# A hybrid decoder layer on one core: where weight slots and activations begin, modulo 128 bytes

## The chip, the core and the metric

The kernel runs on one NeuronCore of one Trainium2 chip. The metric is the device time of one execution in microseconds, as a median of runs. The engines are TensorE (PE, with its weight loads shown apart as PEld), VectorE (DVE), ScalarE (ACT), GpSimd (POOL, here only a queue for DMAs) and SyncE (SP, the other DMA queue).

## The reference, cut to what matters

One layer on a prompt of 2048 tokens and on 32 sample tokens, width 1024, all float32:

```
h = rms_norm(x, g_mix_pre);  z = h @ w_in                      # 1024 -> 2048
y_a, y_b, y_c, y_d = pool(z), conformer_conv(z), spatial_gating(z), short_conv(z)
o = concat(y_a, y_b, y_c, y_d) @ w_out                         # 1024 -> 1024
x = x + rms_norm(o, g_mix_post)
f = rms_norm(x, g_ffn_pre)
f = square(relu(f @ w_up)) @ w_down                            # 1024 -> 4096 -> 1024
x = x + rms_norm(f, g_ffn_post)
```

The results are the new x for both token groups and the last rows that each mixer keeps.

## The kernel before, in words

The tokens go in four blocks b of 512; the last block also takes the 32 sample tokens (544 columns). Every weight matrix goes in panels of 256 columns, 1024 rows deep (K = 8 row tiles k of 128), 1 MB each. The list `order` names all panels j in the order in which every engine goes through them. There are 32 I panels (stage 1: w_in, eight per block), and then for each block four O panels (w_out) and four quarters q, each with four U panels (w_up) and four D panels (w_down). Between blocks the first D panel of the last quarter and the O panels of the next block are interleaved.

Products are made in three passes. A float32 weight is split into w_hi (ACT, `split_hi`, L677) and w_lo = raw - w_hi (DVE, `split_lo`, L1127), an activation into act_hi and act_lo (or u_hi and u_lo, the squared-ReLU result). `three` (L1773 to L1775) issues hi x hi, hi x lo and lo x hi into one PSUM bank; every matmul has its own weight load. What stands in the array (the second argument) and what moves over it (the third) depends on the panel:

- In I panels (but for the last) and in U panels w stands, 128 columns of it, and act moves: 512 columns, or 256 and 288 in the last block's U panels.
- In D panels u stands, 128 tokens of it, and w moves, 256 columns. In O panels act stands and w moves. In the last I panel of a block, called VV, and in the sample rows that each I panel of block 0 ends with, act stands and w moves too.

There are two weight slots, panel j uses slot j % 2, and a slot is filled again when panel j - 2 is done. In block 0 of stage 1 the two halves of w_in are also written to DRAM (L610, L611), and blocks 1 to 3 load them from there by POOL's queue (L619, L620), w_hi and w_lo of a panel one after the other. In all other panels the raw weight is loaded by SP and split.

The mixers' results come back from DRAM as mixc, and `mix_part` writes them into act_hi (ACT, L900) and act_lo (DVE, L1432) for the O panels. In block 0 ACT waits there for tiles of the last VV panel, which still reads act. The normalised f then overwrites act for the U panels.

Of the kernel before, what the change touches and what calls it, by code (L numbers as in the profile page):

```python
# [5 lines left out]
def hybrid_trunk_step(nc, x_prompt, x_sample, state_pool, state_conv, state_short, g_mix_pre, g_mix_post,  # L6
# [7 lines left out]
    fp32, f32r, bf16 = mybir.dt.float32, mybir.dt.float32r, mybir.dt.bfloat16  # L14
# [85 lines left out]
    with ctx:  # L100
# [12 lines left out]
        wlo_d = nc.dram_tensor("wlo_scratch", [NI, P, K, PC], f32r, kind="Internal").ap()  # L113

        raw = sb("raw", [P, 2, K, PC])
        w_hi = sb("w_hi", [P, 2, K, PC], f32r)
        w_lo = sb("w_lo", [P, 2, K, PC], f32r)
        ident = sb("ident", [P, P])
        cst = sb("cst", [P, NROW])
        eps = sb("eps", [P, 1])  # L120
# [4 lines left out]
        sgu_gb = sb("sgu_gb", [NS, PC])  # L125
        wpool = sb("wpool", [P, 2, P])
        headmean = sb("headmean", [P, P])
        inv_cnt = sb("inv_cnt", [P, 2, HP + 1])
        v_small = sb("v_small", [P, 3, 4 * NCH])
        vs_small = sb("vs_small", [NS, 3, 4])  # L130

        junk = sb("junk", [P, D], bf16)
        junk_o = sb("junk_o", [P, PC], bf16)
        junk_y = sb("junk_y", [P, PC], bf16)
        warm = sb("warm", [P, 1])
        x_stats = sb("x_stats", [P, 3, NCH])
        xms, xroot, xinv = (x_stats[:, i, :] for i in range(3))


        act_hi = sb("act_hi", [P, K, NX], f32r)  # L140
        act_lo = sb("act_lo", [P, K, NX], f32r)


        sms = sb("sms", [NS, 3])
        oms = sb("oms", [P, NCH + 1, NP])
        osum = sb("osum", [P, NCH + 1])
# [59 lines left out]
        us_sb = sb("us_sb", [P, 2, NS], to=p1)  # L206
        bs_sb = sb("bs_sb", [P, 2, NS], to=p1)
        gate_s = sb("gate_s", [P, 2, NS], to=p1)
        s_gate = v_raw[:, :, :].rearrange("p a c -> p (a c)").rearrange("p (t n) -> p t n", t=2)

        sgu_w_sb = v_n[:, 0:2, :].rearrange("p a c -> p (a c)").rearrange("p (h t) -> p h t", h=4)
# [323 lines left out]
        def _(pool):  # L535
# [71 lines left out]

            for j in range(NI):
                pool.wait_ge(lo_ready, split_no[j])
                pool.dma_start(whi_d[j], w_hi[:, j % 2, :, :]).then_inc(parts_out[j % 2], 16)  # L610
                pool.dma_start(wlo_d[j], w_lo[:, j % 2, :, :]).then_inc(parts_out[j % 2], 16)  # L611
            store(0, 0, ya_done, pool_d[:, :, :])
            for j in part_no:
                _, b, _, p = order[j]
                s = j % 2
                wait_panel(pool, j - 2)
                if j in (NI, NI + 1):
                    pool.wait_ge(parts_out[s], 32 * (NI // 2))
                pool.dma_start(w_hi[:, s, :, :], whi_d[p]).then_inc(part_full[s], 16)  # L619
                pool.dma_start(w_lo[:, s, :, :], wlo_d[p]).then_inc(part_full[s], 16)  # L620
# [47 lines left out]
        def _(act):  # L668
            def split_hi(j):
                if j >= NPAN:  # L670
                    return
                s = j % 2
                act.wait_ge(raw_full[s], 16 * raw_no[j])
                wait_panel(act, j - 2)
                if 2 <= j < NI:
                    act.wait_ge(parts_out[s], 32 * (j // 2))
                SC.activation(w_hi[:, s, :, :], raw[:, s, :, :], ACT.Copy).then_inc(hi_ready, 1)  # L677

            def x_stat(n):

# [211 lines left out]
            def mix_part(b, i):  # L892
                m = no(b, i)
                _, t0, n = tiles_of(b)[i]
                act.wait_ge(mix_full[m % 2], 16 * (m // 2 + 1))
                if b == 0:
                    act.wait_ge(tile_done, 2 * J2 - 1 + i // 2)
                else:
                    wait_panel(act, index("U", b - 1, Q - 1, NP - 1))
                SC.activation(act_hi[:, :, t0:t0 + n], mixc[:, m % 2, :, 0:n], ACT.Copy).then_inc(mix_hi, 1)  # L900

            def o_squares(j, i):
                _, b, _, p = order[j]
# [215 lines left out]
        def _(dve):  # L1119
            def split_lo(j):  # L1120
                if j >= NPAN:
                    return
                s = j % 2
                dve.wait_ge(hi_ready, split_no[j])
                if 2 <= j < NI:
                    dve.wait_ge(parts_out[s], 32 * (j // 2))
                DVE.tensor_tensor(w_lo[:, s, :, :], raw[:, s, :, :], w_hi[:, s, :, :].bitcast(fp32), ALU.subtract)\  # L1127
# [300 lines left out]
            def mix_part(b, i):  # L1428
                m = no(b, i)
                _, t0, n = tiles_of(b)[i]  # L1430
                dve.wait_ge(mix_hi, m + 1)
                DVE.tensor_tensor(act_lo[:, :, t0:t0 + n], mixc[:, m % 2, :, 0:n],  # L1432
                                  act_hi[:, :, t0:t0 + n].bitcast(fp32), ALU.subtract).then_inc(mix_lo, 1)

            def o_copy(j, i):
                _, b, _, p = order[j]
# [334 lines left out]
        def _(pe):  # L1771
# [139 lines left out]
            for b in range(NB):  # L1911
                for jj in range(NI):
                    j, s = NI * b + jj, jj % 2
                    wait_weights(j)
                    for t in range(2):
                        bank = mm[2 * s + t]
                        if jj >= 2:
                            pe.wait_ge(frees[jj], 2 * b + t + 1)
                        elif b > 0:
                            pe.wait_ge(frees[jj], 2 * (b - 1) + t + 1)  # L1920
                        if jj != VV:
                            if jj == 0 and t == 0:
                                pe.wait_ge(h_hi_ready, 2 * NCH * (b + 1))
                                pe.wait_ge(h_lo_ready, 2 * NCH * (b + 1))
                            c = slice(t * P, (t + 1) * P)
                            for k in range(K):
                                last_mm = three(bank[:, :], w_hi[:, s, k, c], w_lo[:, s, k, c],
                                                act_hi[:, k, 0:N1], act_lo[:, k, 0:N1], k)
                            last_mm.then_inc(tile_done, 1)
                            if b == 0 and jj == 0 and t == 0:  # L1930
                                small_parts()
                            if b == NB - 1 and jj == UV and t == 0:
                                last_rows()
                        else:
                            for half in range(2):
                                n = 2 * t + half
                                r = slice(n * P, (n + 1) * P)
                                for k in range(K):
                                    last_mm = three(bank[:, half * PC:(half + 1) * PC], act_hi[:, k, r],
                                                    act_lo[:, k, r], w_hi[:, s, k, :], w_lo[:, s, k, :], k)  # L1940
# [8 lines left out]
                    if b == 0:  # L1949
                        if jj == 0:  # L1950
                            pe.wait_ge(smp_hi, 1)
                            pe.wait_ge(smp_lo, 1)
                            pe.wait_ge(bias_ready, 1)
                        if jj >= 2:
                            pe.wait_ge(zs_ready, jj - 1)
                        for k in range(K):
                            last_mm = three(mm[4 + s][0:NS, 0:PC], act_hi[:, k, N1:NX], act_lo[:, k, N1:NX],
                                            w_hi[:, s, k, :], w_lo[:, s, k, :], k)
# [85 lines left out]
            for j in range(J2, NPAN):  # L2044
# [3 lines left out]
                if kind == "U":  # L2048
# [4 lines left out]
                    for t in range(2):  # L2053
                        c = slice(t * P, (t + 1) * P)
                        for c0, c1 in halves(b):
                            bank = take_bank(j, i)
                            for k in range(K):
                                last_mm = three(mm[bank][:, 0:c1 - c0], w_hi[:, s, k, c], w_lo[:, s, k, c],
                                                act_hi[:, k, c0:c1], act_lo[:, k, c0:c1], k)
                            last_mm.then_inc(bank_done[bank], 1)  # L2060
                            i += 1
                else:
                    hi, lo = (act_hi, act_lo) if kind == "O" else (u_hi, u_lo)
                    for i, bank_tiles in enumerate(token_banks(b)):
                        bank = take_bank(j, i)
                        for h, (tile, t0, n) in enumerate(bank_tiles):
                            for k in range(K):
                                if kind == "O" and p == 0 and k == 0:
                                    pe.wait_ge(mix_lo, no(b, tile) + 1)
                                if kind == "D" and p == 0 and i == 0 and h == 0:  # L2070
                                    pe.wait_ge(u_lo_ready, u_no(b, q, k, len(halves(b))))
                                last_mm = three(mm[bank][0:n, h * PC:(h + 1) * PC], hi[:, k, t0:t0 + n],
                                                lo[:, k, t0:t0 + n], w_hi[:, s, k, :], w_lo[:, s, k, :], k)
# [61 lines left out]
```

## Time and profile before

| | |
|---|---|
| median of 3 runs | 2232.03 us (2230.04 to 2232.41) |
| profiled execution | 2230.47 us, its span 2228.2 us |
| granted TensorE clock, mean | 0.983 |
| PE busy | 2122.0 us (95%), 14425 instructions |
| PEld busy | 1932.4 us (87%) |
| DVE busy | 1083.2 us (49%) |
| ACT busy | 754.6 us (34%) |
| DMA | 287.42 MB, mean 129 GB/s |

The span runs from the first to the last recorded instruction, and the execution's own time is 2.3 us longer. A matmul's duration in the records includes the time in which it drains while the next one is already under way, so a stream of matmuls is measured by the distance of their starts. A few matmul records can be missing, which does not move the starts of the others.

### The profile page before, as it was taken

What the parts mean: (1) busy time and instruction counts of PE and PEld (TensorE: products, weight loads), DVE (VectorE), ACT (ScalarE), POOL (GpSimd) and SP (SyncE); (2) the same over time, 40 slices, a digit from 0 to 9 for tenths busy, and PEclk for the clock granted to TensorE, in tenths of its full rate; (3) what the DMA queues carried; (4) which work ended last, traced back from release to release, by engine and by line L of the source; (5) the groups of instructions that cost most, each with busy time, mean ns of one, the idle gap of its engine ahead of it and who ended that gap; (6) DMA issues with size and microseconds to landing.
All of it is one profiled execution on the core that took longest, in us unless ns stands there. A gap on an engine that the chain in (4) does not pass through costs nothing.

```text
span 2228.2 us, 33002 instructions
## 1 busy us (share of the span) xinstructions
PE 2122.0 (95%) x14425; PEld 1932.4 (87%) x14425; DVE 1083.2 (49%) x1404; ACT 754.6 (34%) x1159; POOL 107.6 (5%) x190
## 2 busy tenths in 40 slices
PE   6999999994999999999999999999999989999997
PEld 5887778784798898989899898889899989999997
DVE  3687786866523334563333346533334553333334
ACT  4424232234233223443322344332324432314132
POOL 2011111110000000000000000000000000000000
PEclk9999999997899999999999999999999999999999
DMA  7754646553132223444233344533334333222231
GB/s 250 277 201 165 222 170 209 194 178 129 59 114 95 95 95 114 139 150 153 94 107 95 97 132 152 170 95 95 95 95 135 108 103 116 77 93 78 77 95 41
DMA packets 184836, 287.42 MB, mean 129 GB/s; under 512 B 5967, under 2 KB 162292, under 8 KB 176484
## 3 DMA queue, kind: packets, MB, share of 16 engines
q1 hardware_dynamic: 160868, 169.99, 23.9%
q0 software_dynamic: 22784, 114.28, 14.6%
q8 instruction: 114, 1.87, 0.3%
q10 hardware_dynamic: 1040, 1.05, 0.1%
q14 instruction: 30, 0.25, 0.0%
HBM read 245.01 MB, written 40.57 MB: 128 GB/s over the span
## 4 chain that ended last, share of the span: by engine, by line
PE 83%; DVE 7%; ACT 4%; DMA 3%; issue 2%; POOL 0%; ACTq 0%; POOLq 0%; DVEq 0%
PE mm L1773 27%; PE mm L1775 27%; PE mm L1774 27%; ACT w_hi L677 2%; DVE w_lo L1127 2%; DMA mixc<-mixT_scratch 1%; DVE conv L1171 1%; PE tr L1778 1%; DMA x_in<-in_x_prompt 1%; DMA raw<-in_w_in 1%; PE tr L2002 1%; ACT junk_y L976 0%; PE mm L1833 0%; PE tr L1799 0%; DVE f_sb L1516 0%
## 5 line engine op out<-in xcount | busy, mean ns | idle before, releaser
L1127 DVE TENSOR_TENSOR w_lo<-raw,w_hi 128x2048 fp32r<-128x2048 f32 x152 | 348.4, 2292 | 696.4 <-ACT w_hi L677 696.4
L1773 PE MATMUL mm<-act_hi,w_hi 128*128 128x512 f32 (+2 forms) x1728 | 632.2, 366 | 11.1 <-DVE act_lo L1484 5.8
L1775 PE MATMUL mm<-act_hi,w_lo 128*128 128x512 f32 (+2 forms) x1728 | 632.3, 366 | 0.0
L1774 PE MATMUL mm<-act_lo,w_hi 128*128 128x512 f32 (+2 forms) x1728 | 625.9, 362 | 0.0
L1773 PE MATMUL mm<-w_hi,u_hi 128*128 128x256 f32 (+1 forms) x2176 | 603.2, 277 | 1.7 <-DVE u_lo L1500 0.9
L1774 PE MATMUL mm<-w_lo,u_hi 128*128 128x256 f32 (+1 forms) x2176 | 600.8, 276 | 0.0
L1775 PE MATMUL mm<-w_hi,u_lo 128*128 128x256 f32 (+1 forms) x2176 | 600.8, 276 | 0.0
L677 ACT ACTIVATE w_hi<-raw 128x2048 fp32r<-128x2048 f32 x152 | 290.8, 1913 | 579.1 <-PE mm L1775 572.9
L1773 PEld LDWEIGHTS mm<-w_hi,u_hi 128*128 128x128 f32 (+1 forms) x2176 | 398.2, 183 | 4.9 <-DVE u_lo L1500 3.8
L1774 PEld LDWEIGHTS mm<-w_lo,u_hi 128*128 128x128 f32 (+1 forms) x2176 | 398.3, 183 | 1.1
L1775 PEld LDWEIGHTS mm<-w_hi,u_lo 128*128 128x128 f32 (+1 forms) x2176 | 398.2, 183 | 0.7
L1773 PEld LDWEIGHTS mm<-act_hi,w_hi 128*128 128x128 f32 x1728 | 328.3, 190 | 62.9 <-issue 14.9
L1774 PEld LDWEIGHTS mm<-act_lo,w_hi 128*128 128x128 f32 x1728 | 328.2, 190 | 57.1 <-issue 2.4
L1775 PEld LDWEIGHTS mm<-act_hi,w_lo 128*128 128x128 f32 x1728 | 327.5, 190 | 50.5
L1773 PE MATMUL mm<-w_hi,act_hi 128*128 128x256 f32 (+1 forms) x736 | 205.9, 280 | 7.0 <-DVE act_lo L1432 4.3
L1774 PE MATMUL mm<-w_lo,act_hi 128*128 128x256 f32 (+1 forms) x736 | 203.9, 277 | 0.0
L1775 PE MATMUL mm<-w_hi,act_lo 128*128 128x256 f32 (+1 forms) x736 | 203.9, 277 | 0.0
L949 ACT ACTIVATE square<-mm 128x512 f32<-128x512 f32 (+2 forms) x160 | 81.8, 511 | 257.7 <-PE mm L1775 255.1
L1171 DVE SCALAR_TENSOR_TENSOR conv<-g_ext,cst,conv 128x512 f32<-128x512 f32 x240 | 163.0, 744 | 0.7 <-ACT conv L800 0.7
L1498 DVE CAST u_hi<-square 128x512 fp32r<-128x512 f32 (+2 forms) x160 | 60.0, 375 | 187.6 <-ACT square L951 187.6
L1773 PEld LDWEIGHTS mm<-w_hi,act_hi 128*128 128x128 f32 (+1 forms) x736 | 131.2, 178 | 9.4 <-issue 5.1
L1774 PEld LDWEIGHTS mm<-w_lo,act_hi 128*128 128x128 f32 (+1 forms) x736 | 131.2, 178 | 2.0 <-issue 0.5
(244 smaller groups left out, 1341.7 us busy)
## 6 DMA issues: line engine op xcount, KB each, us to landing
raw<-in_w_ffn_up SPq DMA_DIRECT2D x64, 1024.0 KB, 5.4
raw<-in_w_ffn_down SPq DMA_DIRECT2D x64, 1024.0 KB, 5.2
w_hi<-whi_scratch POOLq DMA_DIRECT2D x24, 1024.0 KB, 5.2
w_lo<-wlo_scratch POOLq DMA_DIRECT2D x24, 1024.0 KB, 7.9
raw<-in_w_out SPq DMA_DIRECT2D x16, 1024.0 KB, 5.2
whi_scratch<-w_hi POOLq DMA_DIRECT2D x8, 1024.0 KB, 8.6
wlo_scratch<-w_lo POOLq DMA_DIRECT2D x8, 1024.0 KB, 10.8
mixc<-mixT_scratch POOLq DMA_DIRECT2D x16, 512.0 KB, 5.8
```

Of the source, the lines that this page charges most:

```text
L677: SC.activation(w_hi[:, s, :, :], raw[:, s, :, :], ACT.Copy).then_inc(hi_ready, 1)
L949: SC.activation(square[:, at % 2, 0:c1 - c0], mm[bank][:, 0:c1 - c0], ACT.Relu).then_inc(bank_free[bank], 1)
L1127: DVE.tensor_tensor(w_lo[:, s, :, :], raw[:, s, :, :], w_hi[:, s, :, :].bitcast(fp32), ALU.subtract)\
L1171: DVE.scalar_tensor_tensor(out=c, in0=g_ext[:, t, k:k + N1], scalar=col("conv_w", 2 * k + t), in1=c, op0=ALU.mult, op1=ALU.add).then_inc(c ...
L1498: DVE.tensor_copy(u_hi[:, k, c0:c1], square[:, at % 2, 0:c1 - c0]).then_inc(u_hi_ready, 1)
L1773: PE.matmul(out, whi, xhi, start=(k == 0), stop=False)
L1774: PE.matmul(out, whi, xlo, start=False, stop=False)
L1775: return PE.matmul(out, wlo, xhi, start=False, stop=(k == K - 1))
L1778: PE.matmul(bank[:, 0:n], headmean[:, :], src, start=True, stop=True).then_inc(done, 1)
L2002: last = PE.transpose(tr[hh][:, kk * P:kk * P + n], f_sb[0:n, m % 2, k * P:(k + 1) * P], ident[0:n, 0:n])
```

## The change

The change gives each panel's weights an address within their slot by the panel's kind, and gives act two addresses within its buffer, one for the stage in which it moves and one for the O panels, in which it stands. A slot becomes 2064 elements (8256 bytes) per partition instead of 2048, an act buffer 4368 instead of 4352. Six small tensors are allocated at another place, so that act_hi begins at 0 and act_lo at 64 modulo 128. One wait of `mix_part` in block 0 asks for a tile more, since the shifted tile reaches 64 bytes into its neighbour. The diff, without the lines that only put `w_hi(j)` for `w_hi[:, s, :, :]` and `mix_act_hi` for `act_hi`:

```diff
-        w_hi = sb("w_hi", [P, 2, K, PC], f32r)
-        w_lo = sb("w_lo", [P, 2, K, PC], f32r)
+        PITCH = K * PC + P // 8
+        w_hi_slots = sb("w_hi", [P, 2 * PITCH], f32r)
+        w_lo_slots = sb("w_lo", [P, 2 * PITCH], f32r)
...
-        inv_cnt = sb("inv_cnt", [P, 2, HP + 1])
-        v_small = sb("v_small", [P, 3, 4 * NCH])
-        vs_small = sb("vs_small", [NS, 3, 4])
...
+        act_hi_buf = sb("act_hi", [P, K * NX + P // 8], f32r)
+        act_lo_buf = sb("act_lo", [P, K * NX + P // 8], f32r)
+
+        act_hi, mix_act_hi = (act_hi_buf[:, o:o + K * NX].rearrange("p (k t) -> p k t", k=K) for o in (0, P // 8))
+        act_lo, mix_act_lo = (act_lo_buf[:, o:o + K * NX].rearrange("p (k t) -> p k t", k=K) for o in (P // 8, 0))
+
+        def in_slot(slots, j):
+
+            base = (j % 2) * PITCH
+            off = base + (-base if order[j][0] in "OD" else P // 8 - base) % (P // 4)
+            return slots[:, off:off + K * PC].rearrange("p (k c) -> p k c", k=K)
+
+        def w_hi(j):
+            return in_slot(w_hi_slots, j)
+
+        def w_lo(j):
+            return in_slot(w_lo_slots, j)
...
         x_stats = sb("x_stats", [P, 3, NCH])
         xms, xroot, xinv = (x_stats[:, i, :] for i in range(3))
-
-
-        act_hi = sb("act_hi", [P, K, NX], f32r)
-        act_lo = sb("act_lo", [P, K, NX], f32r)
...
-                SC.activation(w_hi[:, s, :, :], raw[:, s, :, :], ACT.Copy).then_inc(hi_ready, 1)
+                SC.activation(w_hi(j), raw[:, s, :, :], ACT.Copy).then_inc(hi_ready, 1)
...
-                    act.wait_ge(tile_done, 2 * J2 - 1 + i // 2)
+
+                    act.wait_ge(tile_done, 2 * J2 - 1 + min(i, 1))
...
-                SC.activation(act_hi[:, :, t0:t0 + n], mixc[:, m % 2, :, 0:n], ACT.Copy).then_inc(mix_hi, 1)
+                SC.activation(mix_act_hi[:, :, t0:t0 + n], mixc[:, m % 2, :, 0:n], ACT.Copy).then_inc(mix_hi, 1)
...
-                    hi, lo = (act_hi, act_lo) if kind == "O" else (u_hi, u_lo)
+                    hi, lo = (mix_act_hi, mix_act_lo) if kind == "O" else (u_hi, u_lo)
```

Where the operands of a matmul begin, in bytes modulo 128, in the two built programs (a row of w is 1024 bytes, a row of act or u 2176 = 17 x 128, and every tile within a row begins at a multiple of 512, so the same offset holds for all tiles):

| panel | before: moves, stands | changed: moves, stands |
|---|---|---|
| I but for VV, U | act 64, w 0 | act 0, w 64 |
| VV, and the sample rows of stage 1 | w 0, act 64 | w 64, act 0 |
| O | w 0, act 64 | w 0, act 64 |
| D | w 0, u 64 | w 0, u 64 |

On every engine the instructions, their order and the semaphores that they wait for are the same in both programs; only addresses differ, and the value of the one wait.

## Rows read from the trace of the kernel before

**Rows 1.** The page, parts 2 (40 slices) and 4 (the chain).
```profile
PEclk9999999997899999999999999999999999999999
...
PE mm L1773 27%; PE mm L1775 27%; PE mm L1774 27%; ACT w_hi L677 2%; DVE w_lo L1127 2%; DMA mixc<-mixT_scratch 1%; DVE conv L1171 1%; PE tr L1778 1%; DMA x_in<-in_x_prompt 1%; DMA raw<-in_w_in 1%; PE tr L2002 1%; ACT junk_y L976 0%; PE mm L1833 0%; PE tr L1799 0%; DVE f_sb L1516 0%
```

**Rows 2.** Groups by form, L1773: form, xcount | busy us, mean ns | idle before.
```profile
L1773 PE MATMUL mm<-w_hi,u_hi 128*128 128x256 f32 x2048 | 567.9, 277 | 1.7 <-DVE u_lo L1500 0.9
...
L1773 PE MATMUL mm<-act_hi,w_hi 128*128 128x512 f32 x1216 | 484.4, 398 | 6.9 <-DVE act_lo L1160 5.3 <-DVE act_lo L1484 1.6
...
L1773 PE MATMUL mm<-w_hi,act_hi 128*128 128x256 f32 x640 | 179.3, 280 | 7.0 <-DVE act_lo L1432 4.3 <-DVE w_lo L1127 2.7
...
L1773 PE MATMUL mm<-act_hi,w_hi 128*128 128x288 f32 x256 | 75.2, 294 | 0.0
...
L1773 PE MATMUL mm<-act_hi,w_hi 128*128 128x256 f32 x256 | 72.5, 283 | 4.2 <-DVE act_lo L1484 4.2
```

**Rows 3.** PE in order of time (start, us): four U panels, first and last of 192.
```profile
1062.04 0.39 PE L1773 MATMUL mm<-act_hi,w_hi 128*128 128x512 f32 x1
...
1105.96 0.39 PE L1775 MATMUL mm<-act_hi,w_lo 128*128 128x512 f32 x1
```

**Rows 4.** Busy PE, PEld, DVE, ACT, POOL, clock, DMA, GB/s: four U panels.
```profile
1062.04:1106.19 44.15, 44.15 (x194) 36.07 (x193) 16.74 (x18) 16.42 (x19) 0.00 (x0) 1.00 0.30 96
```

**Rows 5.** PE in order of time: one D panel, first and last of 96.
```profile
1894.34 0.28 PE L1773 MATMUL mm<-w_hi,u_hi 128*128 128x256 f32 x1
...
1905.11 0.28 PE L1775 MATMUL mm<-w_hi,u_lo 128*128 128x256 f32 x1
```

**Rows 6.** The same: last block's U panel, 24 of 288 and 24 of 256.
```profile
1910.74 0.29 PE L1773 MATMUL mm<-act_hi,w_hi 128*128 128x288 f32 x1
...
1913.91 0.28 PE L1773 MATMUL mm<-act_hi,w_hi 128*128 128x256 f32 x1
...
1916.60 0.28 PE L1775 MATMUL mm<-act_hi,w_lo 128*128 128x256 f32 x1
```

**Rows 7.** The same: 24 of the sample rows, and 48 of VV.
```profile
69.06 0.28 PE L1773 MATMUL mm<-w_hi,act_hi 128*32 128x256 f32 x1
...
71.68 0.28 PE L1775 MATMUL mm<-w_hi,act_lo 128*32 128x256 f32 x1
...
128.62 0.28 PE L1773 MATMUL mm<-w_hi,act_hi 128*128 128x256 f32 x1
...
133.95 0.28 PE L1775 MATMUL mm<-w_hi,act_lo 128*128 128x256 f32 x1
```

**Rows 8.** DVE in order of time.
```profile
476.95 1.22 DVE L1432 TENSOR_TENSOR act_lo<-mixc,act_hi 128x1024 fp32r<-128x1024 f32 x1
...
481.75 1.22 DVE L1189 TENSOR_TENSOR v_n<-v_raw,v_small 128x1024 f32<-128x1024 f32 x1
```

**Rows 9.** POOL and PE in order of time, and landing times of the page, part 6.
```profile
215.48 0.53 POOL L619 DMA_DIRECT2D w_hi<-whi_scratch  x1 [12.26 <-PE mm L1775]
...
228.31 0.79 PE L1773 MATMUL mm<-act_hi,w_hi 128*128 128x512 f32 x1
...
w_lo<-wlo_scratch POOLq DMA_DIRECT2D x24, 1024.0 KB, 7.9
...
raw<-in_w_in SPq DMA_DIRECT2D x7, 1024.0 KB, 9.2
```

**Rows 10.** ACT in order of time, end of stage 1.
```profile
464.54 0.60 ACT L702 ACTIVATE v_raw<-mm 128x512 f32<-128x512 f32 x1 [4.84 <-PE mm L1775]
465.03 1.99 ACT L900 ACTIVATE act_hi<-mixc 128x1024 fp32r<-128x1024 f32 x2
```

**Rows 11.** Waits of DVE in stage 1: us in total, times, longest.
```profile
DVE g_ext L1280 <- ACT p_raw L702: 28.8, 6, 6.1
```

**Rows 12.** Waits of PE from 560 us on.
```profile
PE tr L2002 <- DVE act_lo L1484: 6.2, 6, 1.9
...
PE tr L1778 <- DVE conv_s L1679: 2.6, 1, 2.6
```

More of the change, by code:

```diff
@@ L208, in hybrid_trunk_step @@
         gate_s = sb("gate_s", [P, 2, NS], to=p1)
+        inv_cnt = sb("inv_cnt", [P, 2, HP + 1], to=p1)
+        v_small = sb("v_small", [P, 3, 4 * NCH], to=p1)
+        vs_small = sb("vs_small", [NS, 3, 4], to=p1)
         s_gate = v_raw[:, :, :].rearrange("p a c -> p (a c)").rearrange("p (t n) -> p t n", t=2)
@@ L609, in _ @@
                 pool.wait_ge(lo_ready, split_no[j])
-                pool.dma_start(whi_d[j], w_hi[:, j % 2, :, :]).then_inc(parts_out[j % 2], 16)
-                pool.dma_start(wlo_d[j], w_lo[:, j % 2, :, :]).then_inc(parts_out[j % 2], 16)
+                pool.dma_start(whi_d[j], w_hi(j)).then_inc(parts_out[j % 2], 16)
+                pool.dma_start(wlo_d[j], w_lo(j)).then_inc(parts_out[j % 2], 16)
             store(0, 0, ya_done, pool_d[:, :, :])
@@ L618, in _ @@
                     pool.wait_ge(parts_out[s], 32 * (NI // 2))
-                pool.dma_start(w_hi[:, s, :, :], whi_d[p]).then_inc(part_full[s], 16)
-                pool.dma_start(w_lo[:, s, :, :], wlo_d[p]).then_inc(part_full[s], 16)
+                pool.dma_start(w_hi(j), whi_d[p]).then_inc(part_full[s], 16)
+                pool.dma_start(w_lo(j), wlo_d[p]).then_inc(part_full[s], 16)
                 if p == 0:
@@ L1126, in split_lo @@
                     dve.wait_ge(parts_out[s], 32 * (j // 2))
-                DVE.tensor_tensor(w_lo[:, s, :, :], raw[:, s, :, :], w_hi[:, s, :, :].bitcast(fp32), ALU.subtract)\
+                DVE.tensor_tensor(w_lo(j), raw[:, s, :, :], w_hi(j).bitcast(fp32), ALU.subtract)\
                    .then_inc(lo_ready, 1)
@@ L1431, in mix_part @@
                 dve.wait_ge(mix_hi, m + 1)
-                DVE.tensor_tensor(act_lo[:, :, t0:t0 + n], mixc[:, m % 2, :, 0:n],
-                                  act_hi[:, :, t0:t0 + n].bitcast(fp32), ALU.subtract).then_inc(mix_lo, 1)
+                DVE.tensor_tensor(mix_act_lo[:, :, t0:t0 + n], mixc[:, m % 2, :, 0:n],
+                                  mix_act_hi[:, :, t0:t0 + n].bitcast(fp32), ALU.subtract).then_inc(mix_lo, 1)
             def o_copy(j, i):
@@ L1926, in _ @@
                             for k in range(K):
-                                last_mm = three(bank[:, :], w_hi[:, s, k, c], w_lo[:, s, k, c],
+                                last_mm = three(bank[:, :], w_hi(j)[:, k, c], w_lo(j)[:, k, c],
                                                 act_hi[:, k, 0:N1], act_lo[:, k, 0:N1], k)
@@ L1939, in _ @@
                                     last_mm = three(bank[:, half * PC:(half + 1) * PC], act_hi[:, k, r],
-                                                    act_lo[:, k, r], w_hi[:, s, k, :], w_lo[:, s, k, :], k)
+                                                    act_lo[:, k, r], w_hi(j)[:, k, :], w_lo(j)[:, k, :], k)
                                 if half == 1:
@@ L1957, in _ @@
                             last_mm = three(mm[4 + s][0:NS, 0:PC], act_hi[:, k, N1:NX], act_lo[:, k, N1:NX],
-                                            w_hi[:, s, k, :], w_lo[:, s, k, :], k)
+                                            w_hi(j)[:, k, :], w_lo(j)[:, k, :], k)
                         last_mm.then_inc(zs_done, 1)
@@ L2057, in _ @@
                             for k in range(K):
-                                last_mm = three(mm[bank][:, 0:c1 - c0], w_hi[:, s, k, c], w_lo[:, s, k, c],
+                                last_mm = three(mm[bank][:, 0:c1 - c0], w_hi(j)[:, k, c], w_lo(j)[:, k, c],
                                                 act_hi[:, k, c0:c1], act_lo[:, k, c0:c1], k)
@@ L2072, in _ @@
                                 last_mm = three(mm[bank][0:n, h * PC:(h + 1) * PC], hi[:, k, t0:t0 + n],
-                                                lo[:, k, t0:t0 + n], w_hi[:, s, k, :], w_lo[:, s, k, :], k)
+                                                lo[:, k, t0:t0 + n], w_hi(j)[:, k, :], w_lo(j)[:, k, :], k)
                             if h == len(bank_tiles) - 1:
```

## The prediction

> **What bounds the kernel now.** I read the page first. TensorE's granted clock is at nine tenths or more in 38 of 40 slices [rows 1]; in a stage of four U panels it is 1.00, the 2.4 GHz level, with PE busy all of it [rows 4]. The chain that ended last is 81% matmuls of three lines, L1773 to L1775 [rows 1]. So the kernel is worth what one matmul is worth, times their number. The groups by form, the second view, give that number: each of the three lines issues (L1773 shown) 1216 matmuls of 512 moving columns with act moving, 256 of 288 and 256 of 256 columns with act moving, 2048 of 256 columns with a weight moving over u, and 640 with a weight moving over act [rows 2]. The duration there (398 or 277 ns) overlaps with the next matmul and is no cost. The cost is the pitch, from one start to the next, which is read in the order of time.
>
> Pitch, third view, each from two starts and the matmuls between them:
> - D panel (w moves from offset 0 modulo 128, u stands at 64), 96 matmuls of 256 columns: (1905.11 - 1894.34) / 95 = 113.4 ns [rows 5].
> - U panels (act moves from 64, w stands at 0), 192 matmuls of 512 columns: (1105.96 - 1062.04) / 191 = 229.9 ns [rows 3].
> - U panels of the last block, same offsets: 256 columns (1916.60 - 1913.91) / 23 = 117.0 ns, 288 columns (1913.91 - 1910.74) / 24 = 132.1 ns [rows 6].
> - VV panel of stage 1 (w moves from 0, act stands at 64), 48 matmuls: (133.95 - 128.62) / 47 = 113.4 ns. Sample rows (w moves from 0, a stationary tile of only 32 columns), 24: (71.68 - 69.06) / 23 = 113.9 ns [rows 7].
>
> Here is the pattern on which the forecast rests. 512 columns cost 229.9 = 2 x 113.4 + 3.2. 256 columns from offset 64 cost 117.0 = 113.4 + 3.6. 288 columns: 113.4 x 288/256 = 127.5, and 4.6 more. So a matmul that moves from 0 costs 113.4 ns per 256 columns and nothing fixed, and one that moves from 64 costs the same per column and 3 to 5 ns more, once. The size of the standing tile does not matter (113.9 at 32 columns, 113.4 at 128). Nothing else waits in these stretches: PE is busy 44.15 of 44.15 us [rows 4].
>
> **The change part by part.**
> 1. U panels and the first seven columns of stage 1 (w_hi, w_lo stand, act moves). Standing goes from 0 to 64, moving from 64 to 0. That is the pair of offsets that the D panels already have. By the pattern the fixed part goes. 512 columns: 3 x 1216 = 3648 matmuls x 3.2 ns = 11.7 us. 256 columns in the last block: 768 x 3.6 ns = 2.8 us. 288 columns: 768 x 4.6 ns = 3.5 us. Together 18.0 us. The saving at 512 columns with act from 0 is in no row of before. It is bounded below by nothing (the pitch has to do with the form and not the offset), above by a price per column: if a column from 0 cost only what the 2.4 GHz level asks, 0.417 ns, and 113.4 - 106.7 = 6.7 ns were fixed, then 512 columns would take 220.0 ns and each saves 9.9 ns, 36.1 us in all. I take 3.2, since the step from 256 to 512 columns from offset 64 (229.9 - 117.0 = 112.9) is already what 256 columns from offset 0 cost as a whole.
> 2. The VV panel of each block in stage 1, and the sample rows of stage 1. The slot is chosen by the kind of panel, and these are of kind I though the weight moves in them. So here w moves from 64 and act stands at 0: the worse pair. VV is 4 panels x 4 tiles x 8 x 3 = 384 matmuls, the sample rows 8 x 8 x 3 = 192; 576 x 3.2 = 1.8 us lost.
> 3. O and D panels. w moves from 0 and the stationary (the shifted copy of act, or u) stands at 64, as before: no change, and these are more than half of all, 3 x 2048 for D and 3 x (640 - 128) for O without the sample rows [rows 2]. The transposes and head statistics read tiles that keep their offsets.
> 4. ACT's and DVE's splits now write at 64 for I and U panels. A DVE operation of 1024 elements takes 1.22 us on act and mixc, at offset 64, and 1.22 us on v_raw and v_n, at offset 96 [rows 8], so I take no change. They lie beside a panel of 48 x 0.23 = 11 us and take some 2 us each, which hides a tenth more as well; uncovered, a tenth would be 0.2 us in each of the panels.
> 5. POOL's loads of w_hi and w_lo in stage 1 write 8 KB rows that begin at 64. A pair is issued from 215.48 on, and its panel begins at 228.31: 12.8 us for what takes 0.5 + 7.9 = 8.4 [rows 9]. Some 4 us of slack hide it. No row shows a load that begins at 64; the nearest are w_in's 1 MB loads in the crowded first stage at 9.2 us [rows 9], 1.3 longer, also hidden. I take 0.
> 6. The new wait: in block 0 ACT's second mixing tile waits for one more tile of the last VV panel. Behind it on ACT are two more such tiles, and DVE and the first O panel wait for them. But ACT evacuates that very tile into v_raw at 464.54, ahead of both, and starts the two at 465.03 [rows 10]. The wait is fulfilled when it is reached: 0.
> 7. What a faster PE meets. In stage 1 DVE waits for what ACT takes from PE's results (28.8 us before g_ext alone [rows 11]), so it follows. PE's own waits for DVE from 560 us on are small, the largest 6.2 us in six parts at the block edges [rows 12]; they hang on chains that begin with the end of a PE panel, so they move and do not grow. Only where DVE itself is the chain (the step from block 0 to 1, and the 2.6 us before conv_s [rows 12]) a faster panel becomes a longer wait: 48 + 40 matmuls x 3.2 ns, 0.3 us.
>
> Sum: 18.0 - 1.8 - 0.3 = 15.9 us saved. The profiled execution took 2230.5 us (span 2228.2 and 2.3 around it): 2214.6. The median of the runs is 2232.0, 1.6 above the profiled one, so the forecast is 2216.2.
>
> A rule that speaks against this, in sentences that the sum does not use. The Trainium skill, "TensorE: Matmul & The Clock Gate", section "Back-to-back issue gap", gives a warm pitch of N/2.4 + 2.5 ns with no term for an address: 215.8 ns at 512 columns, where the trace has 229.9, and 109.2 at 256, where it has 113.4 and 117.0. By that rule the sum would be 0; the trace does not agree with it in either form. "SBUF — State Buffer", section "DMA port swizzle", puts the memory's lines at 16 bytes: offsets 64 and 0 would both begin a line and the change would give nothing. The 3 to 5 ns between forms of equal width [rows 5 and 6] are not what that rule leads one to expect, but the forms differ in more than the offset, so it is rival 2 below.
>
> **Rivals.**
> 1. The offset costs per column, not once. Then 512 columns go to 220.0 ns (36.1 us), 256 save 2.8, 288 columns go to 113.4 + 32 x 0.417 = 126.7 (5.5 x 768 = 4.2): 43.1 - 1.8 - 0.3 = 41.0 us, 2191. For it: TensorE at the full level needs no more per column. Against it: 288 columns from 64 cost 4.6 extra and 512 cost 3.2, which does not grow with width.
> 2. The 3 ns belong to the form and not the offset. In rows 5 and 7 a weight moves (1 KB rows), in rows 3 and 6 act moves (rows of 2176 bytes). In this kernel of before, form and offset never part, so no row excludes it. Then nothing changes: 2232, or 2234 if VV alone pays. A change that does not do what it says would end here too.
> 3. Slower: the loads of stage 1 decide. 24 pairs have to land within 12.8 us and take 8.4. Rows that begin in mid-line would have to stretch them 1.5-fold before anything shows; at 1.9-fold, 16.0 us, each pair holds PE 3.2 us, 24 x 3.2 = 77, less the 16 saved: 2293. At 1.65-fold, 13.9 us, it is 26 - 16 = 10 us slower, 2242. Against it: even the crowded loads are below the limit. Nothing speaks for it but that no row shows it.
>
> **How the numbers follow.** My forecast 0.60 (2212 to 2221 for its own range: the 3.2 can't be read better than by some 0.5 ns, and the 3.6 and 4.6 by 0.6). Rival 1 0.12, rival 2 0.18, rival 3 or some other loss 0.10. The range from 2190 to 2233 holds the forecast, rival 1 with what lies between, and most of rival 2; it leaves out rival 3 and the rest of rival 2, whose two ends (2232 and 2234) lie about its edge. A measurement of this kernel tells 0.2%, 4.5 us, from no change: faster 0.72, same 0.18, slower 0.10.
>
> **What would show it.** In the profile after: 192 matmuls of 512 columns in a U stage at a pitch of 226.7 ns (229.9 again is rival 2, 220 rival 1); 256 and 288 columns in the last block at 113.4 and 127.5; D and O unchanged at 113.4; the VV panel up to 116.6 and the sample rows with it (unchanged there, and the standing offset or the form has a part in it). POOL's pairs landing above 12 us, or PE waiting at the head of stage 1's panels, would be rival 3. I am wrong if the pitch of U stays, or if it falls and the waits at the block edges grow by as much.

## The result: slower by 1.3%, and the profile after

The changed kernel takes 2260.28 us (median of 4 runs, 2258.81 to 2262.45) against 2231.03 us of the kernel before in the same series (median of 4 runs): a ratio of 1.0132, with a 95% interval of 1.0114 to 1.0149. The forecast was 2216.2 us with a range of 2190 to 2233. It was wrong in its sign.

These lines of the changed kernel's page give its busy times and granted clock. They answer to the table of times and to [rows 1]:

```profile
span 2258.2 us, 33002 instructions
...
PE 2157.9 (96%) x14425; PEld 1958.8 (87%) x14425; DVE 1083.3 (48%) x1404; ACT 754.4 (33%) x1159; POOL 107.6 (5%) x190
...
PEclk9999999997999999999999999999999999999999
```

The same instructions ran, and DVE, ACT and POOL took the same time for them. PE alone was busy longer: 2157.9 - 2122.0 = 35.9 us. Its idle time shrank from 106.2 to 100.3 us, and 35.9 - 5.9 is the 30.0 us by which the span grew. So nothing new is waited for. The granted clock is no reason either, since its mean rose a little, from 0.983 to 0.985. The matmuls themselves follow each other more slowly. The largest group by form, the matmuls of the D panels, shows it faintly, since durations overlap (line, form, count | busy, mean ns | idle before; it answers to the first row of [rows 2]):

```profile
L1791 PE MATMUL mm<-w_hi,u_hi 128*128 128x256 f32 x2048 | 573.9, 280 | 0.9
```

The starts show it fully. Below is PE of the changed kernel (start and duration, us), the first and last matmul of each stretch: four U panels (192, as [rows 3]), one D panel (96, as [rows 5]), 24 of 288 and 24 of 256 columns in the last block ([rows 6]), a VV panel (48) and sample rows (24, both [rows 7]):

```profile
1072.90 0.39 PE L1791 MATMUL mm<-act_hi,w_hi 128*128 128x512 f32 x1
...
1117.24 0.39 PE L1793 MATMUL mm<-act_hi,w_lo 128*128 128x512 f32 x1
...
1903.68 0.28 PE L1791 MATMUL mm<-w_hi,u_hi 128*128 128x256 f32 x1
...
1914.77 0.28 PE L1793 MATMUL mm<-w_hi,u_lo 128*128 128x256 f32 x1
...
1934.52 0.29 PE L1791 MATMUL mm<-act_hi,w_hi 128*128 128x288 f32 x1
...
1937.56 0.30 PE L1793 MATMUL mm<-act_hi,w_lo 128*128 128x288 f32 x1
1937.69 0.28 PE L1791 MATMUL mm<-act_hi,w_hi 128*128 128x256 f32 x1
...
1940.44 0.29 PE L1793 MATMUL mm<-act_hi,w_lo 128*128 128x256 f32 x1
...
130.06 0.28 PE L1791 MATMUL mm<-w_hi,act_hi 128*128 128x256 f32 x1
...
135.60 0.28 PE L1793 MATMUL mm<-w_hi,act_lo 128*128 128x256 f32 x1
...
69.69 0.28 PE L1791 MATMUL mm<-w_hi,act_hi 128*32 128x256 f32 x1
...
72.39 0.28 PE L1793 MATMUL mm<-w_hi,act_lo 128*32 128x256 f32 x1
```

The next table has the pitch, that is the distance of two starts, before and after. "By the pitch" is its change times the number of matmuls.

| stretch | before, ns | after, ns | matmuls | forecast, us | by the pitch, us |
|---|---|---|---|---|---|
| D and O | 113.4 | 116.7 | 8160 | 0 | +27 |
| U and I, 512 columns | 229.9 | 232.1 | 3648 | -11.7 | +8 |
| U, 256 columns | 117.0 | 119.6 | 768 | -2.8 | +2 |
| U, 288 columns | 132.1 | 132.2 | 768 | -3.5 | 0 |
| VV | 113.4 | 117.9 | 384 | +1.2 | +1.7 |
| sample rows of stage 1 | 113.9 | 117.4 | 192 | +0.6 | +0.7 |

(For instance D: (1914.77 - 1903.68) / 95 = 116.7.) The last column adds up to 39.4 us, but the span grew by 30.0 only. Of the difference, 5.9 us is the idle time that PE lost: a slower stream arrives later at a point at which PE waited anyway. The rest, by an estimate, is in the clock. For short stretches both traces have a granted clock of 0.50, the 1.2 GHz level, where 512-column matmuls start (261.68 - 259.54) / 5 = 428 ns apart instead of 230:

```profile
259.54 0.63 PE L1773 MATMUL mm<-act_hi,w_hi 128*128 128x512 f32 x1
...
261.68 0.63 PE L1775 MATMUL mm<-act_hi,w_lo 128*128 128x512 f32 x1
```

In the changed kernel less of PE's work fell into such stretches. From 500 to 620 us, for instance, the granted clock (third value from the end) was 0.82 before, which is the first of these rows, and 0.84 after, which is the second:

```profile
500.00:620.00 120.00, 85.84 (x475) 73.32 (x475) 72.37 (x154) 45.18 (x81) 6.94 (x11) 0.82 0.26 89
500.00:620.00 120.00, 86.32 (x482) 72.83 (x479) 73.09 (x152) 46.68 (x80) 6.92 (x11) 0.84 0.28 91
```

Over the whole span PE was busy at the 1.2 GHz level for 32.6 us before and for 26.9 us after. By an estimate from these two numbers, half of the 5.7 us came back, 2.9 us. The sum is then 39.4 - 5.9 - 2.9 = 30.6 us, against 30.0 measured. The largest term is one that the forecast had at zero: panels whose operands keep their offset modulo 128.

What does not keep its value is the address modulo 256. The addresses of w_hi and w_lo, of act_hi and act_lo, and of u_hi and u_lo in the two built programs give this table, where k is the row tile:

| modulo 256 | before | changed, slot 0 | changed, slot 1 |
|---|---|---|---|
| D, O: w_hi, w_lo (move) | 128, 128 | 128, 0 | 0, 128 |
| D: u_hi, u_lo (stand), even k | 192, 192 | 192, 192 | 192, 192 |
| U, I: w_hi, w_lo (stand) | 128, 128 | 192, 64 | 192, 64 |
| U, I: act_hi, act_lo (move), even k | 192, 192 | 0, 128 | 0, 128 |

(Rows of act and u are 8.5 x 256 bytes, so at odd k they lie 128 further.) The weight buffers became 16512 bytes, an odd multiple of 128, so w_lo and w_hi no longer agree modulo 256. In D and O panels, where w moves, they are 128 apart.

### The profile page after: what moved, and what is told of

It is laid out like the page before. It is cut to its first block, busy times and chain, and to the rows that moved or that the text cites. A ratio compares the mean times of both kernels' runs of the same rounds, so it can differ in the third digit from the quotient of the medians.

```text
span 2258.2 us, 33002 instructions
## 1 busy us (share of the span) xinstructions
PE 2157.9 (96%) x14425; PEld 1958.8 (87%) x14425; DVE 1083.3 (48%) x1404; ACT 754.4 (33%) x1159; POOL 107.6 (5%) x190
## 4 chain that ended last, share of the span: by engine, by line
PE 85%; DVE 7%; ACT 4%; DMA 2%; issue 2%; POOL 0%; ACTq 0%; DVEq 0%; POOLq 0%
PE mm L1791 28%; PE mm L1792 28%; PE mm L1793 27%; DVE w_lo L1145 1%; ACT w_hi L694 1%; DMA mixc<-mixT_scratch 1%; DVE conv L1189 1%; PE tr L1796 1%; DMA raw<-in_w_in 1%; DMA x_in<-in_x_prompt 1%; PE tr L2020 0%; PE mm L1851 0%; PE tr L1817 0%; ACT junk_y L994 0%; DVE o_sb L1484 0%
## 5 line engine op out<-in xcount | busy, mean ns | idle before, releaser
L1792 PE MATMUL mm<-act_lo,w_hi 128*128 128x512 f32 (+2 forms) x1728 | 632.4, 366 | 0.0
L1791 PE MATMUL mm<-w_hi,u_hi 128*128 128x256 f32 (+1 forms) x2176 | 609.6, 280 | 0.9
L1792 PE MATMUL mm<-w_lo,u_hi 128*128 128x256 f32 (+1 forms) x2176 | 607.8, 279 | 0.0
L1792 PEld LDWEIGHTS mm<-w_lo,act_hi 128*128 128x128 f32 (+1 forms) x736 | 131.6, 179 | 2.2 <-issue 0.5
```

The lines of the kernel that those rows point to most:

```text
L1791: PE.matmul(out, whi, xhi, start=(k == 0), stop=False)
L1792: PE.matmul(out, whi, xlo, start=False, stop=False)
```

## The experiments

### The streams alone, and each part of the change alone

**m1_pairs** leaves the layer out and has no engine but TensorE at work while the streams run. Its core follows, with `at` giving a place by its byte address, and two of the 52 lines of its table (columns, standing columns, moving hi, lo and row pitch, standing hi, lo and row pitch, step, groups):

```diff
+            ('D before s0', 256, 128, 32896, 49280, 1024, 169920, 187328, 2176, 512, 4),
+            ('D after s0', 256, 128, 32896, 49408, 1024, 169920, 187328, 2176, 512, 4),
...
+                        last = three(bank[0:m, 0:n], at(sh + g % 4 * step + k * s_p, m),
+                                     at(sl + g % 4 * step + k * s_p, m),
+                                     at(mh + k * mp, n), at(ml + k * mp, n), k)
```

> A program of TensorE streams alone: it copies one block of x over the whole SBUF and then issues the three-pass pattern of a D or a U panel for 52 choices of the four operands' addresses; nothing of the layer is computed. Each stream is four groups of 24 matmuls (two at 512 columns). Theory A (the pitch depends only on the operands' addresses, and the address modulo 256 counts: the kernel before has w_hi and w_lo both at 128 modulo 256, the changed one has one at 0 and one at 128): the streams with the addresses of before run at 113.4 (D) and 229.9 ns (U), those of the changed kernel at 116.8 and 232.2, and w_lo moved alone by 128 bytes gives 116.8, by 256 bytes 113.4. Rival B (the slower pitch is an effect of the whole program, of other engines or of instruction supply): all D streams have one pitch and no address changes it. Rival C (only the offset modulo 128 of what moves counts, as the prediction had it): w_lo at +64 costs, at +128 it does not.

PE of m1 in order of time, first and last of 96 (the first is followed late, after 200 ns): D with the addresses of before, D with those of the changed kernel, D with w_lo 256 bytes further, D with both halves of w 64 bytes further:

```profile
48.15 0.36 PE L115 MATMUL mm<-mem 128*128 128x256 f32 x1
...
59.03 0.28 PE L117 MATMUL mm<-mem 128*128 128x256 f32 x1
...
70.19 0.36 PE L115 MATMUL mm<-mem 128*128 128x256 f32 x1
...
81.36 0.28 PE L117 MATMUL mm<-mem 128*128 128x256 f32 x1
...
240.01 0.36 PE L115 MATMUL mm<-mem 128*128 128x256 f32 x1
...
250.89 0.28 PE L117 MATMUL mm<-mem 128*128 128x256 f32 x1
...
318.12 0.36 PE L115 MATMUL mm<-mem 128*128 128x256 f32 x1
...
329.50 0.28 PE L117 MATMUL mm<-mem 128*128 128x256 f32 x1
```

The stretches last 10.88, 11.17, 10.88 and 11.38 us. Without the first three matmuls the pitches are, in ns (256-column D streams, then 512-column U streams; each operand moved by so many bytes from the addresses of before; slots 0 and 1 are the two weight slots):

```
D  as before 113.5 (both slots)   as changed 116.7, 116.7 (slots 0, 1)   32 standing columns 113.5
D  w_lo moved    +16 118.3  +32 118.0  +64 118.8  +96 117.9  +128 116.7  +192 117.8  +256, 512 .. 4096 113.5
D  w_hi and w_lo +16 119.1  +32 118.4  +64 118.9  +128 113.4  +192 118.9  +256 113.3
D  u_hi and u_lo +16 117.8  +32 117.0  +64 118.9  +128 113.6  +192 118.9  +256 113.5
D  u_lo alone    +64 116.6  +128 113.8  +256 113.5
U  as before 230.0, 230.5 (slots)   as changed 232.3 (both)
U  act both -64 232.1  -128 229.8  -192 232.3  -256 230.2;  act_lo -64 231.6  -128 231.1  -256 230.0
U  w both +64 232.3  +128 230.0  +192 232.1  +256 230.0;    w_lo +64 231.8  +128 230.7  +256 230.0
```

The D streams and those of 512 columns repeat the pitch that they have in the kernel, before and after, with nothing else running. Rivals B and C fall: addresses alone make it, and +128 costs. Theory A holds in its numbers (113.5, 116.7, and 113.5 again at 256). The exception is U's 256 columns: 117.8 ns in m1 for the addresses of before and of after alike, but 117.0 and 119.6 in the kernels, where 24 of them alternate with 24 of 288 columns. No run shows whether that is the reason.

**e1_act_only** has only act's half of the change and **e2_slots_only** only the weight slots' half. The core of each edit follows, against the changed kernel. A small unused tensor, left out here, keeps the other addresses in place.

```diff
-        PITCH = K * PC + P // 8
+        PITCH = K * PC
...
-            off = base + (-base if order[j][0] in "OD" else P // 8 - base) % (P // 4)
-            return slots[:, off:off + K * PC].rearrange("p (k c) -> p k c", k=K)
+            return slots[:, base:base + K * PC].rearrange("p (k c) -> p k c", k=K)
```

```diff
-        act_hi_buf = sb("act_hi", [P, K * NX + P // 8], f32r)
-        act_lo_buf = sb("act_lo", [P, K * NX + P // 8], f32r)
+        act_hi = mix_act_hi = sb("act_hi", [P, K, NX], f32r)
+        act_lo = mix_act_lo = sb("act_lo", [P, K, NX], f32r)
```

> Only act's part of the change: act_hi and act_lo at two offsets, the weight slots at the addresses modulo 256 of before (w_hi and w_lo 128, both slots). Theory A (D and O panels slowed since w_hi and w_lo, which move there, no longer agree modulo 256): D and O stay at 113.4 ns; the time lies near before, 2231, or as much above or below as U and I give: with act moving from 0 modulo 128 by the prediction's price 12 to 18 us faster, by the pitch of the changed kernel (232.2 at 512 columns) 8 to 10 us slower. Rival B (a whole-program effect of the change): a part of the 29 us stays in D and O although their operands' addresses are those of before.

> Only the weight slots' part of the change: slots 8256 bytes apart, w_lo's buffer 128 bytes further from w_hi's, act at the addresses of before (64 modulo 128, both halves). Theory A: D and O at 116.8 ns as in the changed kernel, 8160 matmuls x 3.4 ns = 28 us less what waits absorb, so 2250 to 2260 us; U's pitch shows what w standing at 64 does alone. Rival B or an effect of act's placement: D near 113.4 and the time near 2231.

e1: 2232.07 us, a ratio of 1.0001 (0.9991 to 1.0011). e2: 2259.63 us, 1.0125 (1.0109 to 1.0141). The slots alone are the whole loss. PE of e1 in order of time, one O panel of the last block, first and last of 96, and the VV panel of block 0, 48:

```profile
1703.00 0.28 PE L1791 MATMUL mm<-w_hi,act_hi 128*128 128x256 f32 x1
...
1713.76 0.28 PE L1793 MATMUL mm<-w_hi,act_lo 128*128 128x256 f32 x1
...
128.68 0.28 PE L1791 MATMUL mm<-w_hi,act_hi 128*128 128x256 f32 x1
...
134.27 0.28 PE L1793 MATMUL mm<-w_hi,act_lo 128*128 128x256 f32 x1
```

The O panel has 113.3 ns. VV has 118.9; there w still moves from 0, and act now stands at 0 modulo 128. In e2 an O panel and four U panels:

```profile
1720.38 0.28 PE L1790 MATMUL mm<-w_hi,act_hi 128*128 128x256 f32 x1
...
1731.47 0.28 PE L1792 MATMUL mm<-w_hi,act_lo 128*128 128x256 f32 x1
...
660.47 0.39 PE L1790 MATMUL mm<-act_hi,w_hi 128*128 128x512 f32 x1
...
704.81 0.40 PE L1792 MATMUL mm<-act_hi,w_lo 128*128 128x512 f32 x1
```

They have 116.7 and 232.1 ns, both as in the changed kernel. So the 2 ns that U lost also come from the slots. e1's U panels stay at 230.0 (192 from 660.16 to 704.09 us): with act moving from 0 and w standing at 0 there is neither the gain nor the loss that its expectation held possible.

### One buffer, 128 or 256 bytes further

```diff
         w_hi = sb("w_hi", [P, 2, K, PC], f32r)
+        gap = sb("gap", [P, 32])
         w_lo = sb("w_lo", [P, 2, K, PC], f32r)
```

(64 instead of 32 in w_lo_256. In both, three small tensors that the long streams do not read move to another place, so that act, u and all after them stay where they are.)

> The kernel before with one address changed: w_lo's buffer begins 128 bytes further, so w_hi lies at 128 and w_lo at 0 modulo 256, both still at 0 modulo 128; act, u and every offset modulo 128 stay (three small tensors move to make room, no matmul of the long stages reads them). Theory A (m1: the two halves of what moves must agree modulo 256): D and O at 116.7 ns instead of 113.4, 8160 x 3.3 = 27 us, U of 512 columns at 230.7, 3648 x 0.7 = 3 us, less some 4 us that waits absorb: 2255 to 2260, the whole of the changed kernel's loss from 128 bytes. Rival (the second slot's distance of 8320 bytes or the two offsets within the slots cause it): near 2231.

> The same with w_lo's buffer 256 bytes further instead of 128. Theory A: w_hi and w_lo agree modulo 256 again, D at 113.4 and U at 230.0, the time within 0.2% of before, 2231. Rival (any change of the distance between the buffers costs, their 16384 bytes being special): D at 116.7 and 2255 or more.

128 bytes: 2252.08 us, 1.0089 (1.0072 to 1.0106). 256 bytes: 2232.81 us, 1.0001 (0.9991 to 1.0010). PE of w_lo_128, a D panel (96), and of w_lo_256, an O panel (96):

```profile
1911.90 0.28 PE L1775 MATMUL mm<-w_hi,u_hi 128*128 128x256 f32 x1
...
1922.99 0.28 PE L1777 MATMUL mm<-w_hi,u_lo 128*128 128x256 f32 x1
```

```profile
1702.35 0.28 PE L1775 MATMUL mm<-w_hi,act_hi 128*128 128x256 f32 x1
...
1713.12 0.28 PE L1777 MATMUL mm<-w_hi,act_lo 128*128 128x256 f32 x1
```

They have 116.7 and 113.4 ns. A gap of 128 bytes makes 20 of the 29 us, and doubling it takes them back, with the small tensors moved alike in both. So the distance of w_lo from w_hi modulo 256 is shown as their cause. The expectation of 2255 to 2260 was 3 us too high. Its allowance for waits was right; what it lacked is the clock:

```profile
PE 2148.3 (95%) x14425; PEld 1955.2 (87%) x14425; DVE 1083.8 (48%) x1404; ACT 754.7 (34%) x1159; POOL 108.0 (5%) x190
```

With a span of 2250.2 us PE idled 101.9 us, 4.3 less than before, where some 4 were allowed. And PE was busy at the 1.2 GHz level for 24.8 us instead of 32.6, which by half of the difference gives 3.9 us, an estimate.

For the remaining 9 us the pitches give some 8, an estimate. U and I have 230.6 ns here (192 matmuls from 659.98 to 704.02 us) against 232.1 in the changed kernel, which is 5.5 us. U's 256 columns have 116.4 against 119.6 there, 2.5 us. e2 has the 232.1 with act at its old place, so the standing halves of w at +64 and +192 are behind the larger part.

### Is there a rule?

> Again TensorE streams alone, nothing of the layer computed; all rows and tiles keep one address modulo 256 unless said. m1 leaves two readings of the 113.4 and 118.9 ns of a 256-column matmul. Theory A1 (relation): what counts is the distance of moving and standing operand modulo 128; 64 apart gives 113.4 and equal gives 118.9, wherever they lie, and the two moving halves must agree modulo 256. Theory A2 (absolute): the moving operand has to lie at 0 modulo 128 and the standing one at 64. They part at moving 64, standing 0: A1 113.4, A2 118 or so. For 512 columns m1 never went below 229.8, with act's rows of 2176 bytes, which lie by turns at 0 and 128 modulo 256. If that turn costs (theory C), rows of 2048 or 2304 bytes bring 512 columns to 2 x 113.4 = 226.8 ns and 256 columns moved over 2176-byte rows stay at 117 to 118; if 512 columns have 3.2 ns of their own (rival), all row pitches give 230. The number of standing columns has no part in either.

The edit against m1 is another table: all addresses are multiples of 4096 plus the offset named. Pitches in ns follow, with m and s for the offsets of what moves and what stands. A row is as long as its columns unless said, and standing rows have 1024 bytes:

```
256 columns, s0:   m0 120.0  m32 116.6  m64 113.3  m96 120.0  m128 118.6  m160 117.4  m192 113.4  m224 118.4
256 columns, s64:  m0 117.8  m64 119.9  m128 117.7  m192 120.0;  m0 with standing rows of 2176 bytes: 113.8
512 columns, s0:   m0 226.6  m32 233.4  m64 229.1  m128 232.3  m192 233.4
512 columns, s64:  m0 233.4  m64 227.3  m192 233.4
512 columns, m64 s0, moving rows of 2176 bytes: 230.2;  of 2304: 228.9;  of 4096: 229.1
256 columns, m64 s0, moving rows of 2048, 2176, 2304 bytes: 117.8, 116.7, 117.8
288 columns, m64 s0: 132.3, 132.3, 131.6 (rows of 1152, 2176, 2304)
```

Both readings fail. "64 apart is fast" (A1) gives m0 s64 at 113.4; it is 117.8. "Moving at 0, standing at 64" (A2) gives m64 s0 as slow; it is the fastest at 113.3. At 512 columns equal offsets do best (226.6 and 227.3), and 64 apart costs 2 to 7 ns, the opposite of 256 columns. But they have to be equal modulo 256: m128 s0 has 232.3. Theory C fails too: neither 2048 nor 2304 bytes as such bring 226.8. What stays is that the pitch depends on offset, row pitch and width together, within a band of 113.3 to 120.9 and of 226.6 to 233.4 ns. (The 120.9 is m0 s64 with both low halves 128 bytes further.)

> TensorE streams alone, with the addresses of this kernel and of layouts that could be built into it. By m2, 512 columns take 226.6 ns where act's rows are 2048 bytes and act and w agree modulo 128; so act at 128 modulo 256 with rows of 2048 bytes over w at 128: 226.6 (before: 230.0). The VV panel with act there: near 120 (before 113.4), and 113.4 if w is moved to +64. For the last block's 256 and 288 columns m2 gives no rule; if any start of act does better than 117 and 132 it shows here. Rival: m2's 226.6 holds only for addresses that are whole multiples of 4096 as m2's were, and U stays at 229 to 230 here.

m3 has a third table, with this kernel's own addresses. Its 512 columns over w at 128 modulo 256 take, with act's rows of 2048 bytes, 226.8 ns for act at 128 modulo 256, 229.1 at 192, 232.3 at 0 and 233.4 at 64; as before 230.0. The rival, that 226.6 needs round addresses, falls. VV would pay 120.0 with such an act, and 117.8, not 113.4, with w moved by 64. 256 and 288 columns never beat 116.7 and 132.2 with rows of 2176 bytes. With act's rows of 2304 bytes and act at 64 modulo 256 the stream of 256 columns took 113.3; no kernel was built with that layout.

### Two kernels from what was found

**agree_256** keeps the offsets modulo 128 of the change and makes hi and lo agree modulo 256:

```diff
-        w_hi_slots = sb("w_hi", [P, 2 * PITCH], f32r)
-        w_lo_slots = sb("w_lo", [P, 2 * PITCH], f32r)
+        w_hi_slots = sb("w_hi", [P, 2 * K * PC + P // 2], f32r)
+        w_lo_slots = sb("w_lo", [P, 2 * K * PC + P // 2], f32r)
...
-            off = base + (-base if order[j][0] in "OD" else P // 8 - base) % (P // 4)
+            off = base + (-base if order[j][0] in "OD" else P // 8 - base) % (P // 2)
```

> The changed kernel with its offsets modulo 128 kept (what moves at 0, what stands at 64) and the halves made to agree modulo 256: w_hi's and w_lo's buffers 16640 bytes, the second slot at 8448 in O and D panels, act_lo a multiple of 256 bytes from act_hi (two small tensors move to make room). Theory A: all of the 29 us comes back, D and O at 113.4, U at 229.8 as m3's stream of that layout, so within 0.2% of 2232: the offsets modulo 128 as such give U nothing. Rival (the prediction's pattern after all, once the halves agree): U at 226.7 and 2216 to 2220.

2233.06 us, 1.0003 (0.9994 to 1.0012). Four U panels (192) and an O panel (96) of it:

```profile
661.50 0.40 PE L1793 MATMUL mm<-act_hi,w_hi 128*128 128x512 f32 x1
...
705.43 0.40 PE L1795 MATMUL mm<-act_hi,w_lo 128*128 128x512 f32 x1
...
1704.69 0.28 PE L1793 MATMUL mm<-w_hi,act_hi 128*128 128x256 f32 x1
...
1715.45 0.28 PE L1795 MATMUL mm<-w_hi,act_lo 128*128 128x256 f32 x1
```

They have 230.0 and 113.3 ns, the pitches of before. The idea of the change, carried out without its side effect, is worth nothing, and my pattern with it. (VV, where w moves from 64 here, has 113.4 ns, 48 matmuls from 129.87 to 135.20 us.)

**rows_2048** is the kernel before with act packed closely for the U panels of blocks 0 to 2:

```diff
+        act_hi_buf = sb("act_hi", [P, K * NX + 16], f32r)
+        act_lo_buf = sb("act_lo", [P, K * NX + 48], f32r)
...
+        act_hi = act_hi_buf[:, 16:16 + K * NX].rearrange("p (k t) -> p k t", k=K)
+        act_lo = act_lo_buf[:, 0:K * NX].rearrange("p (k t) -> p k t", k=K)
+        f_act_hi = act_hi_buf[:, 0:K * N1].rearrange("p (k t) -> p k t", k=K)
+        f_act_lo = act_lo_buf[:, 48:48 + K * N1].rearrange("p (k t) -> p k t", k=K)
```

> The kernel before with another layout of act for the U panels of blocks 0 to 2 alone: rows of 2048 instead of 2176 bytes, act_hi and act_lo beginning at 128 modulo 256, where w_hi and w_lo begin; stage 1, O panels and the last block keep their addresses. Theory (m3: 226.8 ns at 512 columns with that layout, 230.0 with the old): 2304 matmuls x 3.2 ns = 7.4 us less, 0.3%, so 2224 to 2226. Rival (the rest of the kernel, whose engines and DMAs also read the memory, sets U's pitch): 230.0 as before and 2232. Nothing is waited for in these panels, so all of it should reach the end.

2225.45 us, 0.9968 (0.9956 to 0.9981), the fastest of all. Four of its U panels (192):

```profile
656.61 0.40 PE L1781 MATMUL mm<-act_hi,w_hi 128*128 128x512 f32 x1
...
699.93 0.39 PE L1783 MATMUL mm<-act_hi,w_lo 128*128 128x512 f32 x1
```

(699.93 - 656.61) / 191 = 226.8 ns, as in m3. 2304 x 3.2 = 7.4 us were expected and 2232.18 - 2225.45 = 6.7 came. This forecast rested on a pitch measured at the addresses in question, and held.

## Why the prediction was wrong, point by point

1. *The bound.* Right: PE's pitch times the number of matmuls. The pitches account for 39 of the changed kernel's us; 5.9 went into waits that were there before and, by the estimate above, 2.9 into the clock. The forecast had left the clock out.
2. *The pattern, "a matmul that moves from 0 costs 113.4 ns per 256 columns and nothing fixed, and one that moves from 64 costs the same per column and 3 to 5 ns more, once."* Wrong, and the first step that failed. It was drawn from four streams that differ in offset, width and row pitch at once. The sums agreed to 0.5 ns by chance. As for the pattern, m2 has 512 columns from 0 modulo 128 anywhere between 226.6 and 233.4 ns, and 256 columns from 64 at 113.3. Rival 2 said that form and offset never part in this trace; that should have weighed more than the sum that came out even. Rival 1 did not happen either: 220 ns lie below the fastest 512 columns of any run, 226.6.
3. *"O and D panels ... no change."* The step that cost most: 0 forecast, 27 us by the pitch. The step that failed is the cost per matmul, taken as 113.4 ns before and after; it became 116.7. I compared offsets modulo 128, since the change speaks of those, and took equality there for equality. The built programs had the full addresses, and the distance of w_lo from w_hi had gone from 16384 to 16512 bytes. w_lo_128 and w_lo_256 settle it.
4. *U and stage 1.* -18.0 forecast; +10 by the pitch. agree_256 shows 0 for the offsets as such, e2 that the loss is the slots'.
5. *VV and the sample rows.* +1.8 forecast, +2.4 by the pitch. The sign was right by luck. The reason, moving from 64, was not: e1 makes VV as slow (118.9) with w still moving from 0, and agree_256 moves w from 64 at 113.4 ns.
6. *"The size of the standing tile does not matter."* Right for these addresses (m1: 113.5 at 32 columns). m2 has 116.7 at 32 standing columns where 128 have 117.8 (m0 s64), and 113.3 against 119.9 (m64 s64), so it is no rule.
7. *Splits, POOL's loads, the new wait.* Right. (What a faster PE would meet, the 0.3 us, was not put to the test, since PE became slower.) The splits last what they did in busy time (DVE 1083.3, ACT 754.4 us), and ACT's last evacuation again precedes both mixing tiles. POOL's loads did not decide, so rival 3, the slower one, named the wrong mechanism. Here are ACT and POOL of the changed kernel in order of time, answering to [rows 9, 10]:

```profile
469.88 0.60 ACT L719 ACTIVATE v_raw<-mm 128x512 f32<-128x512 f32 x1 [5.05 <-PE mm L1793]
470.37 1.99 ACT L918 ACTIVATE act_hi<-mixc 128x1024 fp32r<-128x1024 f32 x2
```

```profile
w_lo<-wlo_scratch POOLq DMA_DIRECT2D x24, 1024.0 KB, 7.9
```

8. *The chances.* The pattern got 0.60, though no row had tested it, and all that is slower got 0.10, with the loads by DMA as the only kind that was worked out. A change of addresses whose effect on TensorE I could only extrapolate deserved a rival of the kind "another relation of the same addresses gets worse, in all panels": 8160 matmuls times the 3.6 ns that lie between two streams of 256 columns (117.0 and 113.4, [rows 5 and 6]) is 29 us, a price that the trace of before gave.

## What to carry to other kernels

The pitch of a stream repeats to some 0.3 ns when its addresses do (D as before: 113.5 in m1, 113.8 in m3), so an edit of buffer sizes can be an edit of matmul speed. List the full addresses of all operands of the long streams before and after, not the offsets that the edit is about, and keep what was fast (here w_hi and w_lo equal modulo 256). Do not deduce a rule for addresses from a few streams of a kernel; a program of bare streams at the candidate addresses gave the pitch of D and of 512 columns to 0.5 ns, before, after, for w_lo_128 and for rows_2048. For U's 256 columns it was off by up to 1.8 ns. And a sum of pitches is not yet the time: a slower stream also eats into waits, and the share of the work that runs at the 1.2 GHz level can move by some us.

## What the runs showed of the hardware

- float32r matmuls of 256 columns start 113.3 to 120.9 ns apart, of 512 columns 226.6 to 233.4, at a granted clock of 1.00 and with no other engine at work, by the addresses and row pitches of the moving and standing operands alone. That is up to 6.7% and 3.0%.
- Every shift of w by 256 bytes, alone or together, and of act or u by 256, gave the pitch back within 0.3 ns (m1). With one operand's rows of 2176 bytes, 8.5 x 256, a common shift of both halves of w, u or act by 128 did so too. With closely packed rows it did not: 512 columns went from 226.6 to 232.3 (m2) and from 226.8 to 232.3 (m3). Shifts of 16, 32, 64, 96 and 192 bytes from the placement of before cost 1.6 to 5.7 ns each in m1, of one half of w by 128 bytes 3.2 (256 columns) and 0.7 (512 columns). From the best placements of m2, a shift of 32 bytes cost up to 6.8.
- The best placement depends on the width, with closely packed rows: at 256 columns moving from 64 or 192 over standing at 0 (113.3 and 113.4; the reverse, from 0 over 64, takes 117.8), at 512 columns both equal modulo 256. 288 columns varied less, 131.6 to 133.4.
- TensorE's granted clock was 0.50 for some stretches of each trace, in which 512-column matmuls started 428 ns apart. The slower kernels spent less of PE's busy time there: 26.9 us (changed), 24.4 (e2) and 24.8 (w_lo_128) against 32.6 to 39.5 in the other five. The runs do not show why.
- Why addresses matter is open. Loads of weights and matmuls overlap (PEld is busy for 1932.4 us and PE for 2122.0 of the 2228.2 before), so two reads of the memory run side by side, and that they meet in it would fit; but no run separates the two reads, and the order of effects over offset and row pitch has no simple law in these data.
